# A mixer made token-major on one stacked state, spread maxima products, and modulation tiles on PE

## What is computed

```python
mod = silu(cond) @ ada_w + ada_b                       # modulation
def step(carry, inp):                                  # one chunk of 128 tokens, one head, one direction
    cm, nv, m = carry
    bcum = cumsum(lf)
    dmat = where(causal, bcum[:, None] - bcum[None, :] + li[None, :], NEG)
    inter = m + bcum
    mt = maximum(inter, dmat.max(-1))
    w_inter = exp(inter - mt)
    a = (qc @ kc.T) * exp(dmat - mt)
    num = w_inter * (qc @ cm) + a @ vc
    den = w_inter * (qc @ nv) + a.sum(-1)
    hc = num / maximum(abs(den), exp(-mt))
    m_new = mt[-1]
    w_s, w_c = exp(bcum[-1] - bcum + li - m_new), exp(m + bcum[-1] - m_new)
    return (w_c * cm + (w_s * kc).T @ vc, w_c * nv + (w_s * kc).sum(0), m_new), hc
hm = h_forward + flip(h_backward)
hm = hm * rsqrt(mean(hm * hm, over a head's 128 values) + EPS) * g_mout
m_out = sigmoid(mo) * hm
y = concat([attn, m_out]) @ w_out
```

## Time and profile before

| what | us |
|---|---|
| runs, median of 3 | 2959.61 (2959.53 to 2967.38) |
| profiled execution, its span | 2956.75, 2955.0 |
| PE busy, DVE busy, ACT busy | 2723.0, 1391.1, 908.1 |
| start, until the first modulated input | 53.4 |
| first feed-forward | 511.4 |
| in-projection of the even mixer | 111.4 |
| latent attention | 189.4 |
| mLSTM | 182.0 |
| rest of the out-projection | 56.8 |
| everything behind | 1850.6 |
| a 512 KB weight tile, issue to landing | 3.3 |

### The profile page before, as it was taken

How to read it: one execution, slowest core, us unless ns; L and a number is a source line. 1 busy time by engine, 2 the same in 40 slices (tenths; PEclk the granted TensorE clock), 3 DMA queues, 4 the chain that set the end, 5 groups by cost and what they waited for, 6 DMA issues and landing times.

```text
span 2955.0 us, 41889 instructions
## 1 busy us (share of the span) xinstructions
PE 2723.0 (92%) x17533; PEld 2593.1 (88%) x17549; DVE 1391.1 (47%) x2078; ACT 908.1 (31%) x1255; POOL 6.0 (0%) x7
## 2 busy tenths in 40 slices
PE   3999999898868788999998999999899998999997
PEld 2999999795656588999997999999788897999997
DVE  7888321423356737775223654222555535232212
ACT  3333222434431143222223222222433334333221
POOL 0000000000000000000000000000000000000000
PEclk8999999899977799999999999999999999999999
DMA  5555222120000014553222342222120011222221
...
DMA packets 71332, 255.12 MB, mean 86 GB/s; under 512 B 10572, under 2 KB 11788, under 8 KB 70720
## 3 DMA queue, kind: packets, MB, share of 16 engines
...
## 4 chain that ended last, share of the span: by engine, by line
PE 84%; DVE 10%; ACT 3%; issue 1%; DMA 1%; SPq 1%; DVEq 0%; ACTq 0%
PE ps L1799 71%; PE ps L864 2%; PE ps L548 1%; PE ps L1827 1%; DVE hs L1301 1%; DVE xT L1769 1%; DVE y L1765 1%; PE ps L493 1%; PE ps L850 1%; DVE e_mx L648 1%; DVE w_lo L377 1%; ACT w_hi L371 1%; PE ps L853 1%; PE ps L852 1%; DVE ada_junk L1614 1%
## 5 line engine op out<-in xcount | busy, mean ns | idle before, releaser
L377 DVE TENSOR_TENSOR w_lo<-w_raw,w_hi 128x1024 fp32r<-128x1024 f32 (+1 forms) x284 | 372.9, 1315 | 1095.3 <-ACT w_hi L371 1095.0
L1799 PE MATMUL ps<-hx_hi,w_hi 128*128 128x320 f32 x3488 | 804.1, 312 | 72.4 <-DVE hx_lo L1668 57.1
L1799 PE MATMUL ps<-hx_lo,w_hi 128*128 128x320 f32 x3488 | 801.1, 311 | 0.0
L1799 PE MATMUL ps<-hx_hi,w_lo 128*128 128x320 f32 x3488 | 800.3, 311 | 0.0
L371 ACT CAST w_hi<-w_raw 128x1024 fp32r<-128x1024 f32 (+1 forms) x284 | 317.9, 1122 | 1339.6 <-PE ps L1799 1313.9
L1799 PEld LDWEIGHTS ps<-hx_hi,w_hi 128*128 128x128 f32 x3488 | 589.9, 190 | 77.8 <-issue 60.0
L1799 PEld LDWEIGHTS ps<-hx_lo,w_hi 128*128 128x128 f32 x3488 | 590.2, 190 | 0.0
L1799 PEld LDWEIGHTS ps<-hx_hi,w_lo 128*128 128x128 f32 x3488 | 589.7, 190 | 0.0
L1799 PE MATMUL ps<-hh_hi,w_hi 128*128 128x320 f32 x1408 | 320.8, 309 | 0.0
L1799 PE MATMUL ps<-hh_lo,w_hi 128*128 128x320 f32 x1408 | 320.5, 309 | 0.0
L1799 PE MATMUL ps<-hh_hi,w_lo 128*128 128x320 f32 x1408 | 320.5, 309 | 0.0
...
## 6 DMA issues: line engine op xcount, KB each, us to landing
...
first_a<-in_ada_w SPq DMA_DIRECT2D x10, 512.0 KB, 11.8
...
```

The lines of the kernel that those rows point to most:

```text
L377: nc.vector.tensor_tensor(w_lo[:, slot, 0:tiles * P], w_raw[:, slot, 0:tiles * P], w_hi[:, slot, 0:tiles * P], ALU.subtract).then_inc(lo_d ...
L1799: last = nc.tensor.matmul(ps[:, out_bank + h, 0:TH], w, a[:, k, h * TH:(h + 1) * TH], start=(start and w is wh and a is hi), stop=(stop an ...
```

## The change

- Start: x is loaded first, then the 16 modulation tiles in another order. Tiles 8 to 13 are multiplied on PE against a conditioning column; DVE does the other ten.
- Projection: the last eight weight tiles (v and o) give token-major results `v_m` and `mo`. The gate rows are moved by 20 small DMAs and scanned in gaps of the projection; their columns and floors are made by ACT at its end. Three small loads no longer wait for the input.
- Attention: the unit products stand singly between scores and attend; the rests are made later in the head; the negated maxima are no longer stored.
- mLSTM: five units (context, then one a head), both directions stacked in a state of 128 rows; outputs token-major, so that a denominator is one value a row; the norm and the gate are in the unit, and a transpose ("flip") turns a finished head back. `mlstm_plan` is the list that the engines walk. The out-projection's first products wait for the heads up to the third, and the last head's flip stands before k tile 7.

```diff
+            ahead = units[h + 1][3 * (x - 2):3 * (x - 1)] if x in (2, 3, 4) else []
+            plan += ahead[0:1] + [("scores", h, x)] + ahead[1:2]
             if before:
...
+            if h + 1 < MLA_HEADS and x == (2 if h % 2 == 0 else 5):
+                plan.append(("rest", h + 1, 0))
...
-            if x in (2, 3, 4):
-                plan += units[h + 1][3 * (x - 2):3 * (x - 1)]
+            plan += ahead[2:3]
...
+def mlstm_plan():
+
+    plan = [("front", 0), ("weights", 0), ("gain", 0)]
+    for u in range(CHUNKS):
+        nxt = u + 1 < CHUNKS
+        plan += [("front", u + 1)] * nxt + [("states", u)] + [("flip", u - 1)] * (u > 0) + [("num", u)]
+        plan += [("hi", u - 1)] * (u > 0) + [("weights", u + 1)] * nxt + [("low", u - 1)] * (u > 0)
+        plan += [("gain", u + 1)] * nxt + [("divide", u), ("halves", u), ("sums", u), ("out", u)]
+    return plan + [("flip", CHUNKS - 1), ("hi", CHUNKS - 1), ("low", CHUNKS - 1)]
...
+        first_order = [0, 1, 8, 2, 3, 9, 4, 5, 10, 6, 7, 11, 14, 12, 15, 13]
+        by_pe, by_dve = range(KT, KT + 6), (*range(KT), 14, 15)
...
+            def first_scales():
+                pe.wait_ge(col_ready, 1)
+                for i, j in enumerate(by_pe):
+                    wait_first(pe, j)
+                    for k in range(KT):
+                        ins = nc.tensor.matmul(ps[:, 7, 2 * i:2 * i + 2], ada_first(j)[:, k * P:(k + 1) * P],
+                                               cond_col[:, k, :], start=(k == 0), stop=(k == KT - 1))
+                    ins.then_inc(scale_done, 1)
...
+        def pe_token_major(pe, chunk, which, i):
+
...
+                for k in range(2):
+                    cols = slice(k * 512, (k + 1) * 512)
+                    for a, w in ((hx_hi, w_hi), (hx_hi, w_lo), (hx_lo, w_hi)):
+                        last = nc.tensor.matmul(ps[:, tok_bank(which, c), :], a[:, 2 * i + k, c * P:(c + 1) * P], w[:, q, cols],
+                                                start=i == 0 and k == 0 and a is hx_hi and w is w_hi,
+                                                stop=i == 3 and k == 1 and a is hx_lo)
+                if i == 3 and c < CHUNKS - 1:
...
+            pe_token_major(pe, chunk, 1, 3)
+            pe.wait_ge(l_vfill, 2 * CHUNKS)
+            pe.wait_ge(r_columns, 1)
...
-                sp.wait_ge(hx_ready, 2 * KT)
-                sp.dma_start(tmp[NOPE:MLA_QK, 0, 0:PAST], io["krope_old"]).then_inc(mix_loaded, 16)
...
+        def sp_gate_rows(sp):
+
+            sp.wait_ge(rows_clear, 1)
+            sp.wait_ge(proj_done, 4)
+            for d in range(2):
+                for c in range(CHUNKS):
+                    for j, row in enumerate((R_I, R_F)):
+                        r, g = ml_row(d, 0, c), 8 * d + 4 * j
+                        sp.dma_start(grow[r:r + M_HEADS, row, :],
+                                     gates[g:g + M_HEADS, c * P:(c + 1) * P]).then_inc(gates_moved, 16)
...
+            act.wait_ge(r_turned, 3)
...
+                elif kind == "num":
+                    pe.wait_ge(l_w, u + 1)
+                    pe.wait_ge(l_state, u + 1)
+                    if u:
+                        pe.wait_ge(l_hm, u)
+                    for j in range(4):
+                        h, c = ml_block(u, j)
+                        for d in range(2):
+                            out = ps[:, 4 + j, 129 * d:129 * d + 129]
+                            ins = nc.tensor.matmul(out, decay[:, two, d, j * P:(j + 1) * P], v_m[:, c, h, :],
+                                                   start=(d == 0), stop=(d == 1 and u == 0))
+                            if u:
+                                ins = nc.tensor.matmul(out, q_inter[:, two, j * P:(j + 1) * P], state[:, h, j, d, :],
+                                                       start=False, stop=(d == 1))
+                    ins.then_inc(l_num, 1)
...
+                elif kind == "halves":
+                    act.wait_ge(l_den, u + 1)
+                    for j in range(4):
+                        ins = nc.scalar.activation(hm[:, u, j, :], ps[:, 4 + j, 0:P], ACT.Copy, scale=den[:, two, j, 0:1])
+                    ins.then_inc(l_half, 1)
+                elif kind == "sums":
+                    act.wait_ge(l_sq, u + 1)
+                    link(act, act_chain, nc.scalar.activation(h_ss[:, u, :], h_ss[:, u, :], ACT.Ln, bias=eps_col[:, 0:1],
+                                                              scale=1.0 / M_DV))
+                    nc.scalar.activation(h_ss[:, u, :], h_ss[:, u, :], ACT.Exp, scale=-0.5).then_inc(l_rstd, 1)
...
+                    if u == 1:
+                        dve.wait_ge(mix_loaded3, 32)
+                    for step in range(3):
+                        for d in range(2):
+                            j = step if d == 0 else 3 - step
+                            nxt, rows, a = j + 1 - 2 * d, slice(64 * d, 64 * d + 64), 129 * (j % 2)
+                            last = j * P + (P - 1 if d == 0 else 0)
+                            ins = nc.vector.scalar_tensor_tensor(out=state[rows, h, nxt, d, :], in0=state[rows, h, j, d, :],
+                                                                 scalar=g_inter[rows, two, d, last:last + 1],
+                                                                 in1=ps[rows, 2 + j // 2, a:a + 129], op0=ALU.mult, op1=ALU.add)
+                        if step < 2:
+                            link(dve, dve_chain, ins)
+                    ins.then_inc(l_state, 1)
...
+                    link(dve, dve_chain, nc.vector.tensor_tensor(by, dens, floors[:, u].unsqueeze(3), ALU.max))
+                    link(dve, dve_chain, nc.vector.scalar_tensor_tensor(out=by, in0=dens, scalar=-1.0, in1=by,
+                                                                        op0=ALU.mult, op1=ALU.max))
+                    nc.vector.reciprocal(den[:, two], den[:, two]).then_inc(l_den, 1)
+                elif kind == "halves":
+                    dve.wait_ge(l_half, u + 1)
+                    dve.wait_ge(l_den, u + 1)
+                    for j in range(4):
+                        ins = nc.vector.scalar_tensor_tensor(out=hm[:, u, j, :], in0=ps[:, 4 + j, 129:129 + P],
+                                                             scalar=den[:, two, j, 1:2], in1=hm[:, u, j, :],
+                                                             op0=ALU.mult, op1=ALU.add)
+                    ins.then_inc(l_hm, 1)
+                    dve.wait_ge(l_hm, u + 1)
+                    for j in range(4):
+                        ins = nc.vector.scalar_tensor_tensor(out=junk[:, j, :], in0=hm[:, u, j, :], scalar=1.0, in1=hm[:, u, j, :],
+                                                             op0=ALU.mult, op1=ALU.mult, accum_out=h_ss[:, u, j:j + 1])
+                    ins.then_inc(l_sq, 1)
...
-                        first_products(chunk, lambda t: (o_done, MLA_OUT) if t < 4 else (mix_ready, t - 3))
+                        first_products(chunk, lambda t: (mix_ready, max(t - 2, CHUNKS - 1)),
+                                       lambda: pe_flip(pe, CHUNKS - 1))
```

793 lines of the change are left out of this document (425 added, 368 removed).

## The result

The changed kernel takes 2836.01 us (median of 4 runs, 2832.83 to 2836.72), before 2961.69 (2959.53 to 2967.38): ratio 0.9566, interval 0.9547 to 0.9586. Forecast: 2839, range 2814 to 2866. The profiled execution has a span of 2833.6, that is 121.4 under the 2955.0 of before; the prediction's sum was 120.0. The terms did not all come out as they were priced, so the sum hides errors of opposite sign. The table takes the same points in both traces: the addition of the modulation's bias on VectorE, the last matmul before the projection, its first, its last, attention's first, the end of attention's last subtraction, ScalarE's first split of the out-projection.

The account below looks back on a forecast made before the run. TensorE, busy 92% of the span, was taken to bound most of the kernel, VectorE the start, both handing work over in the mLSTM. Terms -8.7, -2.2, +3.5, -13, -99.6 sum to -120.0: 2839 us, range 2814 to 2866.

Parts of the forecast that it names:

- Start: Kernel start: VectorE multiplies ten modulation tiles instead of sixteen, from 19.6 to 44.5 us; -8.7 us.
- The cover: Start: PE does its six tiles' scales behind VectorE's chain, through at 41 us, costing nothing if done by 44.5.
- In-projection: Projection: shorter gap -1.1, eight token-major weight tiles -1.6, gate rows' transposes +0.5, their DMAs hidden; -2.2 us.
- The gap: Projection: PE's gap of 2.50 us before 570.76 shrinks as a load leaves SP's queue; 1.1 us taken.
- ScalarE before attention: Between projection and attention: two table loads and four exps make PE wait 5.3 us instead of 1.8; +3.5.
- Attention: Attention: spread maxima products remove PE's waits, a new k_top wait costs 1.85 a head; net -13 us.
- a wait under 5: Attention, sign of being right: PE's waits for the maximum, 23.0 us before, fall under 5.
- mLSTM: End of attention to the out-projection's split: five stacked units replace ten, 91.4 us instead of 191.0; -99.6 us.
- A prologue above 25: mLSTM, sign of being wrong: the work before the units' regular steps takes more than 25 us.
- the middle value: mLSTM: a unit takes 13.5 us, between 11.8 with PE at 2.4 GHz and 15.4 at 1.2.
- the 11.8 of the rival: mLSTM: PE stays at 2.4 GHz, a unit takes 11.8 us, 10 less in all, 2829; chance 0.12.
- two clock rivals: mLSTM: PE at 2.4 GHz, 10 us less (2829, chance 0.12), or at 1.2, 13 more (2852, chance 0.16).

Follow-up runs that it names:

- e7: Changed kernel with the gate floors only copied at the projection's end, their four exps moved behind the last table load, in attention; 2825.74 us.
- e1: Changed kernel with the next head's nine maxima products again three and three behind the attend; span 2853.0 us.
- e6: Changed kernel with ScalarE casting the next head's queries one scores step ahead of the head's end; span 2833.6 us.
- e12: Changed kernel with the floors' exps later, the second decay spread written six times and the queries cast early; 2827.65 us.
- e4: Changed kernel with PE writing a unit's second decay spread six times instead of once (units 2 to 4), filling idle time; span 2833.6 us.

## Why the prediction was right, and where not

- **Start.** The chain of ten tiles was right to half a microsecond. The cover was not: PE was through at 42.9 and not at 41, since its clock fell to half in the middle of the scales. I had reasoned that only the first squares would run slowly and the scales not; PE ran quick first and slow afterwards. With 0.8 us to spare the cost stayed nothing.
- **In-projection.** The gap gave 0.94 of the 1.1. The token-major tiles gave 8 x (7.04 - 30 x 0.233) = 0.4 instead of 1.6: a mis-sized term. The transposes of the gate rows took 1.1 between and behind the tiles and not 0.5. The DMAs were hidden as computed, at 0.63 each. That the matmuls behind the gap are no longer slow (0.53 apart before, 0.29 now) I had not priced, 1.4 us by six pairs. Together -0.9 - 0.4 - 1.4 + 1.1 are the -1.6 of the table.
- **ScalarE before attention.** The way grew by 3.0 and not by 3.5. The prediction's 1.8 was PE's idle time, and so counted it is now 4.9 and not 5.3. Its sum was not sound either: the listed pieces are 4.2, and with the whole 1.8 of before they give 6.0. The four exps took 0.42 and not 0.8. That the two loads stand on the path is shown by e7, where it fell by 3.0 without them and the exps. The Trainium skill's drain ("ScalarE: Activation LUTs", section "What ACT_TABLE_LOAD costs") does not show: 662.89 to the first exp at 664.18 and 664.60 to the sigmoid at 665.89 is 1.29 both times, the load alone. The Trainium skill's spacing of 131 ns for 512 columns ("TensorE: Matmul & The Clock Gate", section "Back-to-back issue gap") does not show either, 233 here.
- **Attention.** The sum was near (-15.3 for -13) for other reasons than those given. Idle time fell by 8.2 and not by 13: the waits for the maximum gave 16.6, where I let 3.75 a head go, 26 in all, and one sign that I had named for being right, a wait under 5, did not come (6.4). `k_top` took 9.4 and not 13, six times 1.6. The other 7.0 are the same instructions at a higher clock, for which the sum had no term: 44 us at half clock became 32. The short stretches went with the waits, and e1 brings three back with them (at 738, 758 and 786); but e6 and e12 took the next 5 to 6 us of idle time away and got more time at half clock, 46 and 41. What decides whether a stretch at half clock comes stays open. Nearly half of the time won in attention was thus not the mechanism that I had priced.
- **mLSTM.** The mis-sized term, 95.8 for 99.6, by pieces that came near one by one. Prologue 28.1 for 26, three units 42.7 for 40.5, to the first products 7.9 for 7.5, seven k tiles 12.4 for 13.5, flip and last tile 3.8 for 3.9: 94.9 for 91.4 (the 13.5 were mis-summed, 7 x 1.8 being 12.6). A prologue above 25 had been named as a sign of being wrong. Up to the weights of unit 1 it was 21.2 for 19.5; up to the first output it was the 28.1, but there the sum itself had 26, so the sign was badly set. In the unit, 14.2 for 13.5: states 2.2 for 1.87, weights and low part 4.2 for 3.9, the wait for ACT's half 1.2 for 0.93, squares 0.95 for 1.53, and 2.25 of waiting for PE, the mix of both paces that the middle value stood for. The middle was a choice between two seen paces and not derived, so that it was hit is partly luck. The run e4 shows a unit with all products at 2.4 GHz to be 12.1, near the 11.8 of the rival. The prices of the two clock rivals were not worked out to the end: 1.9 or 1.7 a unit over three units is 5 to 6, and the rest of the 13 and the 10 stands on no row.
- **Not priced.** The 1.6 us before the projection and 0.7 behind the mixer; the first varies from 512.8 to 514.3 in the experiments, and the second lies well within what that stretch varies by, so no cause was looked for.

The forecast's nearness to 2836 is thus partly luck: attention alone, in one and the same program, ran for 168 and for 192 us, with 26.0 and 21.8 us of idle time, the shorter one idle for longer.
